# Expert weights of a routed SwiGLU loaded in 2 KB runs, four rows by 512 columns to a unit

## The reference

```python
D_MODEL = 1024; SEQ = 256; N_EXPERTS = 8; TOP_K = 2; D_FF_EXPERT = 3584

def swiglu(x, w_gate, w_up, w_down):
    return (jax.nn.silu(x @ w_gate) * (x @ w_up)) @ w_down

def moe_swiglu(h, router_w, w_gate, w_up, w_down):
    ...
    logits = (xt @ router_w).astype(jnp.float32)
    top_val, top_idx = lax.top_k(logits, TOP_K)
    gates = jax.nn.softmax(top_val, axis=-1)
    ...
    for e in range(N_EXPERTS):
        y = y + combine[:, e:e + 1] * swiglu(xt, w_gate[e], w_up[e], w_down[e]).astype(jnp.float32)
```

## Time and profile before

| | |
|---|---|
| median of 3 runs | 1593.9 us |
| profiled execution | 1592.31 us, span 1590.5 us |
| PE busy (products) | 1514.3 us, 95% |
| weight loads busy (PEld) | 1328.0 us, 83% |
| DVE, ACT, POOL busy | 16%, 11%, 9% |
| DMA, mean over the span | 433.48 MB, 273 GB/s |
| DMA in the expert stage | 343 to 399 GB/s in slices of 650 to 1560 us |
| TensorE clock | granted in full in all 40 slices (tenths: 9) |

### The profile page before, as it was taken

How to read it: one execution, slowest core, us unless ns; L and a number is a source line. 1 busy time by engine, 2 the same in 40 slices (tenths; PEclk the granted TensorE clock), 3 DMA queues, 4 the chain that set the end, 5 groups by cost and what they waited for, 6 DMA issues and landing times.

```text
span 1590.5 us, 54507 instructions
## 1 busy us (share of the span) xinstructions
PE 1514.3 (95%) x25957; PEld 1328.0 (83%) x25957; DVE 258.1 (16%) x489; ACT 179.0 (11%) x383; POOL 143.4 (9%) x167
## 2 busy tenths in 40 slices
PE   8999999999999999999999999999999999999997
PEld 7787587777687864888999999999998899999996
DVE  3433410000243434100010010010000010000002
ACT  3223220000131332200000000000000000000001
POOL 2243200000022522200000000000000000000000
PEclk9999999999999999999999999999999999999999
DMA  9213344444242145999999999999999999999992
GB/s 338 87 53 133 106 159 159 159 159 146 103 149 107 54 154 189 353 373 356 383 384 371 377 361 377 384 371 371 376 372 366 357 372 382 371 374 361 387 370 95
DMA packets 133612, 433.48 MB, mean 273 GB/s; under 512 B 9082, under 2 KB 33916, under 8 KB 119052
## 3 DMA queue, kind: packets, MB, share of 16 engines
q1 hardware_dynamic: 132384, 427.70, 71.8%
q0 software_dynamic: 672, 2.14, 0.5%
q10 hardware_dynamic: 332, 0.13, 0.0%
HBM read 428.89 MB, written 1.05 MB: 270 GB/s over the span
## 4 chain that ended last, share of the span: by engine, by line
PE 92%; issue 3%; DVE 2%; ACT 1%; POOL 1%; DMA 0%; ACTq 0%; DVEq 0%
PE ps L1126 35%; PE ps L1150 18%; PE ps L975 9%; PE ps L681 8%; PE ps L986 4%; PE ps L844 4%; PE ps L692 3%; PE ps L1183 2%; PE ps L1055 1%; PE ps L801 1%; PE ps L811 1%; PE ps L707 1%; PE ps L714 1%; PE ps L677 1%; PE ps L821 1%
## 5 line engine op out<-in xcount | busy, mean ns | idle before, releaser
L1126 PE MATMUL ps<-AT_sb,ring 128*64 128x88 f32 x5376 | 216.6, 240 | 13.2 <-issue 13.0
L1150 PE MATMUL ps<-LT_sb,ring 128*64 128x88 f32 x5376 | 215.9, 239 | 13.0 <-issue 12.3
L1126 PEld LDWEIGHTS ps<-AT_sb,ring 128*64 128x64 f32 x5376 | 210.7, 138 | 19.0 <-issue 17.0
L1126 PE MATMUL ps<-wpost,ring 128*64 128x88 f32 x5376 | 215.1, 239 | 11.4 <-issue 10.1
L1150 PEld LDWEIGHTS ps<-LT_sb,ring 128*64 128x64 f32 x5376 | 210.8, 137 | 17.4 <-issue 14.9
L1126 PEld LDWEIGHTS ps<-wpost,ring 128*64 128x64 f32 x5376 | 209.7, 138 | 16.3 <-issue 13.5
L975 PEld LDWEIGHTS ps<-hT_sb,ring 128*128 128x128 f32 x768 | 136.0, 190 | 24.6 <-issue 9.1
L975 PE MATMUL ps<-hT_sb,ring 128*128 128x256 f32 (+1 forms) x768 | 155.7, 362 | 0.0
L681 PE MATMUL ps<-hT_sb,ring 128*128 128x256 f32 x592 | 133.4, 383 | 0.0
L681 PEld LDWEIGHTS ps<-hT_sb,ring 128*128 128x128 f32 x592 | 112.4, 192 | 15.9 <-DVE late L1628 0.5
L1972 POOL TENSOR_SCALAR small<-small 128x1 f32<-128x1 f32 x16 | 3.8, 240 | 1196.6 <-ACT late L1506 927.2
(11 more groups left out here) (284 smaller groups left out, 1144.7 us busy)
## 6 DMA issues: line engine op xcount, KB each, us to landing
ring<-in_moe_w_gate SPq DMA_DIRECT2D x84, 1024.0 KB, 8.3
ring<-in_moe_w_up SPq DMA_DIRECT2D x84, 1024.0 KB, 8.1
ring<-in_moe_w_down SPq DMA_DIRECT2D x84, 1024.0 KB, 8.1
late<-in_moe_w_up SPq DMA_DIRECT2D x28, 1024.0 KB, 8.2
late<-in_moe_w_gate SPq DMA_DIRECT2D x28, 1024.0 KB, 7.9
late<-in_moe_w_down SPq DMA_DIRECT2D x28, 1024.0 KB, 8.2
ring<-in_ffn_w_gate SPq DMA_DIRECT2D x11, 1024.0 KB, 5.3
ring<-in_ffn_w_up SPq DMA_DIRECT2D x11, 1024.0 KB, 8.0
```

What stands on the lines that cost most here:

```text
L1126: ins = mm(o[lo:lo + P // 2, :], pairs[:, m % 2, lo:lo + P // 2], xgT[e % 2][:, k, :], start=(k == 0 and m % 4 == 0), stop=(k == KD - 1), ...
L1150: ins = mm(o[lo:lo + P // 2, :], d[:, i, m * P + lo:m * P + lo + P // 2], moe_hid[:, 2 * j + i, :], start=(first and m % 4 == 0), stop=las ...
```

## The change

All units become four 128-row blocks by 512 columns (`RUN`), with 2 KB together in memory. In the 8-tile chunks a gate or up unit now holds half of the columns and four row blocks, where it held all of the columns and two. A down unit holds half of the output columns and four row blocks, where it held all columns and two. Rows are no longer interleaved, so products take neighbouring columns. The number of units, their size, their order by kind, the buffers, the calls for each unit and the tables of turns stay. In the last chunk (4 tiles) gate and up units are what they were.

```diff
@@ -72,6 +72,7 @@
 FIRST_MOE = 2 * N_MIX + FFN_CH
 
 UNIT = 2048
+RUN = 512
 N_OWN = NSLOT * SLOT // UNIT
 N_UNIT = N_OWN + 4
 
@@ -450,16 +451,17 @@
                 return late[:, (i - 6) * UNIT:(i - 5) * UNIT]
             return ring[:, SLOT + (i - 10) * UNIT:SLOT + (i - 9) * UNIT]
 
+        def column_half(c, j):
+
+            return j % 2 if MOE_TILES[c] == 8 else 0
+
         def gate_ks(c, j):
 
-            nk = 2 * 8 // MOE_TILES[c]
-            return range(j * nk, (j + 1) * nk)
-
-        def gate_unit(n, c):
-            return unit_of(n).rearrange("p (k f) -> p k f", f=MOE_TILES[c] * P)
-
-        def down_unit(n):
-            return unit_of(n).rearrange("p (i d) -> p i d", d=D)
+            first = j // 2 * 4 if MOE_TILES[c] == 8 else j * 4
+            return range(first, first + 4)
+
+        def unit_rows(n):
+            return unit_of(n).rearrange("p (r f) -> p r f", f=RUN)
 
         def tiles_of(b, c):
 
@@ -589,16 +591,15 @@
                     else:
                         sp_.wait_ge(unit_used, per_round(r, n - N_UNIT + 1, ROUND_UNITS))
                     if kind == "d":
-                        lo = (MOE_AT[c] + 2 * j) * P
-                        dst = unit_of(n)
-                        src = moe_down[0, e][lo:lo + 2 * P, :].rearrange("(p i) d -> p (i d)", p=P)
+                        lo = (MOE_AT[c] + j // 2 * 4) * P
+                        src = moe_down[0, e][lo:lo + 4 * P, j % 2 * RUN:(j % 2 + 1) * RUN]
                     else:
-                        f = slice(MOE_AT[c] * P, (MOE_AT[c] + MOE_TILES[c]) * P)
+                        lo = MOE_AT[c] * P + column_half(c, j) * RUN
+                        f = slice(lo, lo + RUN)
                         ks = gate_ks(c, j)
-                        dst = gate_unit(n, c)
-                        src = (moe_gate if kind == "g" else moe_up)[0, e][ks.start * P:ks.stop * P, f]\
-                            .rearrange("(k p) f -> p k f", p=P)
-                    sp_.dma_start(dst, src).then_inc(unit_landed[n % N_UNIT], 16)
+                        src = (moe_gate if kind == "g" else moe_up)[0, e][ks.start * P:ks.stop * P, f]
+                    src = src.rearrange("(r p) f -> p r f", p=P)
+                    sp_.dma_start(unit_rows(n), src).then_inc(unit_landed[n % N_UNIT], 16)
 
             moe_loads(0, True)
             sp_.wait_ge(rounds_ready, 1)
@@ -1115,16 +1116,15 @@
                 for j in units_of(c, part):
                     n = UNITS[kind, e, c, j]
                     landed(r, n)
-                    w = gate_unit(n, c)
+                    w, hp = unit_rows(n), column_half(c, j)
                     for i, k in enumerate(gate_ks(c, j)):
                         if kind == "g" and c == 0 and k % 4 == 0:
                             pe.wait_ge(xg_ready, per_round(r, 2 * e + k // 4 + 1, 2 * N_EXP))
-                        for m in range(MOE_TILES[c]):
-                            o = bank(b + m // 4)[:, m % 4 * SLOTS:(m % 4 + 1) * SLOTS]
-                            pairs = w[:, i, m // 2 * 2 * P:(m // 2 + 1) * 2 * P].rearrange("p (f i) -> p i f", i=2)
+                        for m in range(4):
+                            o = bank(b + hp)[:, m * SLOTS:(m + 1) * SLOTS]
                             for lo in (0, P // 2):
-                                ins = mm(o[lo:lo + P // 2, :], pairs[:, m % 2, lo:lo + P // 2],
-                                         xgT[e % 2][:, k, :], start=(k == 0 and m % 4 == 0), stop=(k == KD - 1),
+                                ins = mm(o[lo:lo + P // 2, :], w[:, i, m * P + lo:m * P + lo + P // 2],
+                                         xgT[e % 2][:, k, :], start=(k == 0 and m == 0), stop=(k == KD - 1),
                                          skip_group_check=True)
                                 turned(ins, e, f"{kind}{c}", call)
                                 call += 1
@@ -1141,14 +1141,14 @@
                 for j in units_of(c, part):
                     n = UNITS["d", e, c, j]
                     landed(r, n)
-                    d = down_unit(n)
-                    for i in range(2):
-                        first, last = c == 0 and j == 0 and i == 0, c == MOE_CH - 1 and j == MOE_TILES[c] // 2 - 1 and i == 1
-                        for m in range(KD):
-                            o = bank(4 + m // 4)[:, m % 4 * SLOTS:(m % 4 + 1) * SLOTS]
+                    d = unit_rows(n)
+                    for i in range(4):
+                        first, last = c == 0 and j < 2 and i == 0, c == MOE_CH - 1 and i == 3
+                        for m in range(4):
+                            o = bank(4 + j % 2)[:, m * SLOTS:(m + 1) * SLOTS]
                             for lo in (0, P // 2):
                                 ins = mm(o[lo:lo + P // 2, :], d[:, i, m * P + lo:m * P + lo + P // 2],
-                                         moe_hid[:, 2 * j + i, :], start=(first and m % 4 == 0), stop=last,
+                                         moe_hid[:, j // 2 * 4 + i, :], start=(first and m == 0), stop=last,
                                          skip_group_check=True)
                                 turned(ins, e, f"d{c}", call)
                                 call += 1
```

## The result

| | before | changed |
|---|---|---|
| median, 20 runs each | 1594.97 us | 1612.61 us |
| lowest and highest | 1587.99, 1605.25 | 1601.93, 1617.51 |
| ratio, 95% interval | | 1.0108 [1.0093, 1.0124] |
| span of the profiled execution | 1590.5 us | 1606.9 us |

A forecast was written before the change was run, and what follows sets the result against it. PE was taken to be the bound, stalling when instruction blocks queue behind weight data. Packets 30 us plus extra waits 3 us gave 33 us on the profiled 1592.3 us, 1625.3; forecast median 1626 us, range 1598 to 1652.

The forecast's parts named there:

- my sign of being wrong: Expert stage: PE's "issue" waits should rise from 44.7 to 70 to 85 us; an unchanged sum would refute the forecast.
- The packet term: Expert stage's weight transfers: 2 KB packets lengthen the data queued ahead of PE's instruction blocks; 30 us slower.
- three ways of costing: PE's cost from 0.30 us more data per block: with relief 14 us, by occupancy 34, by cases at hand 41.
- the way with relief: PE's block starts: a stall lets the DMA engines catch up by its own length; 14 us over 170 blocks.
- the relief formula: PE's block starts: with 63 of 170 blocks stalling, s = 0.37 x (0.30 - s), mean stall growth 0.08 us.
- six cases: Block starts with a whole 2 KB pair last in the queue: mean stall 0.50 us against 0.26 overall, giving 41 us.
- The growth of a block's data: Expert stage: a unit costs each DMA engine 0.16 us more, so at 1.88 units a block grows 0.30 us.
- The term of the extra waits: PE's two added waits per expert, uncounted in the tables of turns, make SP's pairs leave later; 0 to 8 us, 3 taken.
- my 16 to 50 us: Whole kernel: the forecast's own band of slowdown, given chance 0.60.
- Packets counted instead of bytes: Rival at instruction fetches: a fixed number of packets goes ahead, so 2 KB packets shorten waits; about 1560 us, chance 0.08.
- Complete relief: Rival in the expert stage: stalls and idle DMA time soak up the 0.30 us; 0 to 16 us, 1602, chance 0.18.
- Weights never came late: Answers the rival that half-row down units land after their use and PE waits for `unit_landed`; 1655 us, chance 0.14.

The follow-up runs named there:

- late marks: Kernel before with SP's pairs released 24 instead of 8 instructions into each instruction block; ratio 1.0098 [1.0068, 1.0127].
- shorter down units: Changed kernel without its two extra waits per expert, each down unit cut to three of its four row blocks; 1574.5 us, 0.9871 [0.9840, 0.9901].
- mark 0: Kernel before with SP's pairs released at the very start of each instruction block instead of 8 instructions in; ratio 1.0220 [1.0186, 1.0253].

## Why the prediction was half right

**The mechanism held.** PE stalls when its instruction block is fetched behind queued weights. Leaving out half of the bytes took the stalls away. The traces show it stall by stall as well: in the kernel before each of the 64 stalls of PE from 642 us on ends 1.2 to 1.6 us after an instruction packet of about 1.0 us has come in. A block of 5.13 us less 1.0 us and the median of 1.4 us leaves the 2.7 us of slack that the prediction had read from one stall. The same distance, but for one stall of 87 at 1.0 us, holds in the changed kernel. The chain stayed at 0% DMA, products kept their 239 to 240 ns, packets doubled, and PE's "issue" waits rose in number. The row I named for the sum of these waits, 70 to 85 us on the products, came out at 51.0, closer to "the sum stays", my sign of being wrong: part of it was the smaller effect, part of it stalls hidden in modelled ends, which the weight loads' rows show.

**The packet term was too large: 30 us taken, 4 us measured** (0.3 to 7.8 us). Two steps of it failed.
- *The choice between three ways of costing.* I gave 14, 34 and 41 us and took 30, against the way with relief. The late marks (0.28) and the shorter down units (0.31) put the price of 1 us of queue per block at what the relief formula has, 0.27, so the 14 us were the way to go. The six cases with a mean stall of 0.50 us were single blocks behind ordinary ones; by the relief formula the next block gives part of such a loss back, which no run isolates.
- *The growth of a block's data.* I put it at 0.30 us. By the price of 0.31, the 4 us stand for 4 / (170 x 0.31) = 0.08 us. By the DMA shares a unit went from 2.76 us to 99.2% x 910 / (329.43 / 1.0486) = 2.87 us, 0.11 us more, which would be 0.21 us a block and 11 us. Part of the error was the sample: 4 KB packets took 173 ns in the mean of 660 to 1500 us, not the 162 ns of one stretch, while 2 KB packets took 89 ns as I had it. The rest is that at 2 KB the share of packet time overstates what a fetch waits for. I had noted shares over 100% as overlap and still costed by them. Why overlap takes up the packets' extra time at 2 KB and not at 1 KB is open.

**The term of the extra waits was too small: 3 us taken, 11 to 13 us measured.** I had 8 us from the formula and took less, on the guess that a queue which is never empty hides a late pair. It does not: 24 instead of 8 instructions cost the formula's 15 us. The lateness itself was as forecast: the count gives 0.07, 0.18 and 0.28 us for the three thirds of the stage, the stalls of the trace 0.12, 0.16 and 0.29 us. At the measured price of 0.28 the mean of 0.19 us is worth 9 us of the 11 to 13; the rest is within the bounds of the measurement and has no cause shown.

The sum 30 + 3 = 33 us stands against 4 + 13 = 17 us: the errors went opposite ways, and the term I called small carried three quarters of the result. That the time still fell inside the range, at the low edge of my 16 to 50 us, was luck.

**The rivals.** Packets counted instead of bytes: no, since shorter packets never made it faster, and with 1 KB packets stalls grew most. The Trainium skill's rule of turns for each packet, "DMA: Bandwidth & Descriptors", section "Queues, rings and completion order", would let a fetch start after one packet whatever is queued. If each packet of the trace is one of these, that is 90 ns, and the 3.6 us of the prediction and the 3.9 us at mark 0 contradict it. But the page counts up to 64 descriptors to a packet. If what the trace lists are descriptors, one packet could last 64 x 90 ns = 5.8 us at 2 KB (an estimate from that page's number), and then 3.6 us of queued data do not disagree with the rule, though the prediction says so. No run here tells the two apart. Complete relief (0 to 16 us) describes the packet term by itself. Weights never came late, not even at 1 KB. And "mostly hidden", as the Trainium skill's page "Runtime: NRT & Kernel Launch", section "Instruction fetch mechanics", has the cost of a new block, holds here at a data share of 59.6% (1.3 us), and not at 94.6% (35.8 us) or more.

## What to carry to other kernels

Where a schedule is counted in instructions, count what a change adds before costing its large part. Two uncounted waits for each expert cost 11 to 13 us, and doubling the packets 4 us (0.3 to 7.8). When a stall gives its own length back to the queue that caused it, price a shift by the share of stalled blocks (here 0.27 to 0.31 us for each us), and more where most blocks stall (0.55 at 1 KB). A DMA share near or over 100% is no safe measure of occupancy: costing by it gave too much at 2 KB and about the right time at 1 KB. Test the amount of data itself.

## What the runs showed of the hardware that was not expected

- Instruction blocks of PE wait behind data that SP has queued: with all data PE lost 60 to 70 us at block starts, with half of it nearly nothing (1526.6 us against 1599.8 us).
- Issuing a pair of 1 MiB transfers about 8 instructions into a block is near the best place of the four tried: 16 later costs 1.0%, 4 sooner may gain 0.2% (interval 0.9954 to 1.0004), 8 sooner costs 2.2%, where the pair goes ahead of the fetch in the trace (3.9 us of data alone).
- Halving runs from 4 and 8 KB to 2 KB cost 0.25%; halving again to 1 KB cost a further 4.7%.
